# One expert scatter in place of two: the halves of a small item's output rows are summed on VectorE first

## What is computed

```python
D_MODEL, SEQ, N_EXPERTS, TOP_K, D_FF = 1024, 512, 32, 4, 1024

def _moe_sequence(h, w_router, b_router, w_gate_up, b_gate_up, w_down, b_down):
    logits = (jnp.einsum('ld,de->le', h, w_router) + b_router).astype(jnp.float32)
    top_val, top_idx = lax.top_k(logits, TOP_K)
    gates = jax.nn.softmax(top_val, axis=-1).astype(h.dtype)
    ...
    xs = h[tok]
    hgu = lax.ragged_dot(xs, w_gate_up, group_sizes) + b_gate_up[e_sorted]
    act = _clamped_swiglu(hgu)
    out = lax.ragged_dot(act, w_down, group_sizes) + b_down[e_sorted]
    out = out * gates.reshape(-1)[order][:, None]
    return jax.ops.segment_sum(out, tok, num_segments=L)
```

## Time and profile before

| | |
|---|---|
| median of 3 runs | 1970.95 us (1967.66 to 1971.95) |
| the profiled execution | 1965.19 us, span 1963.4 us |
| busy, share of the span | PE 95%, DVE 84%, ACT 69%, POOL 23% |
| items 0 to 33 | 743 to 1939 us of the span |
| mean granted TensorE clock | 0.976 of full speed |

### The profile page before, as it was taken

The page is one execution under the profiler, slowest core; times in us unless marked ns, Lnnn a source line. Parts: engine busy times, 40 slices in busy tenths (PEclk is TensorE's granted clock), DMA queues, the critical chain, the costliest instruction groups (busy, mean ns, idle before and its releaser), DMA issues.

```text
span 1963.4 us, 28736 instructions
## 1 busy us (share of the span) xinstructions
PE 1859.5 (95%) x8464; PEld 1450.4 (74%) x8464; DVE 1647.7 (84%) x1766; ACT 1357.9 (69%) x1777; POOL 455.4 (23%) x412
## 2 busy tenths in 40 slices
PE   6999999998989999999999999999999999999897
PEld 3657767787758887877777787677777778777775
DVE  6899987349765478989999998898898999989897
ACT  4556855224345525888788887888888888888885
POOL 6671000000000116412312311321222222212122
PEclk7999999999999998999999999999999999999999
DMA  8222225422110248999999999999999999999995
GB/s 321 81 107 86 86 79 190 138 83 91 34 43 23 47 155 266 355 376 377 368 403 375 373 376 381 366 367 387 368 363 404 374 383 375 391 383 358 399 380 209
DMA packets 134432, 526.22 MB, mean 268 GB/s; under 512 B 15809, under 2 KB 21089, under 8 KB 114208
## 3 DMA queue, kind: packets, MB, share of 16 engines
q1 hardware_dynamic: 118704, 492.45, 66.5%
q0 software_dynamic: 15664, 32.97, 6.5%
HBM read 512.76 MB, written 23.74 MB: 273 GB/s over the span
## 4 chain that ended last, share of the span: by engine, by line
PE 30%; DMA 12%; DVE 7%; ACT 5%; issue 5%; SPq 0%; ACTq 0%; DVEq 0%
PE ps L1135 25%; DMA ring<-in_w_gate_up 8%; DVE split L2826 4%; DMA arena<-in_w_gate_up 3%; PE ps L1184 3%; DVE arena_r L2826 2%; ACT arena_r L2024 2%; ACT split L2024 2%; ACT arena L2049 1%; PE ps L1088 1%; PE ps L1174 1%; DMA arena<-in_w_down 1%; DMA ring<-in_w_down 1%; DVE aTs L2770 0%; ACT arena L2060 0%
## 5 line engine op out<-in xcount | busy, mean ns | idle before, releaser
L1135 PE MATMUL ps<-split,xTs 128*128 128x512 f32 x2016 | 509.9, 401 | 20.3 <-DVE split L2826 14.7
L1135 PEld LDWEIGHTS ps<-split,xTs 128*128 128x128 f32 x2016 | 379.4, 191 | 120.3 <-DVE split L2826 33.4
L2826 DVE TENSOR_TENSOR split<-ring,split 128x2048 fp32r<-128x2048 f32 x136 | 308.2, 2295 | 42.6 <-ACT split L2024 36.9
L2826 DVE TENSOR_TENSOR split<-arena,split 128x2048 fp32r<-128x2048 f32 x136 | 308.7, 2286 | 4.0 <-ACT split L2024 3.6
L2024 ACT ACTIVATE split<-ring 128x1024 fp32r<-128x1024 f32 x272 | 272.5, 1057 | 51.4 <-DMA ring<-in_w_gate_up 47.3
L2024 ACT ACTIVATE split<-arena 128x1024 fp32r<-128x1024 f32 x272 | 272.5, 1052 | 44.8 <-DMA arena<-in_w_gate_up 16.1
L839 POOL DMA_INDIRECT y_rows<-arena,slots x50 | 108.1, 2162 | 336.4 <-issue 299.0
L1135 PE MATMUL ps<-arena_r,xTs 128*128 128x512 f32 x672 | 182.1, 405 | 0.9 <-DVE arena_r L2826 0.4
L1135 PE MATMUL ps<-arena_r,aTs 128*128 128x512 f32 x672 | 170.3, 398 | 0.0
L1135 PE MATMUL ps<-split,aTs 128*128 128x512 f32 x672 | 168.2, 396 | 1.0 <-DVE aTs L2886 0.3
L2826 DVE TENSOR_TENSOR arena_r<-ring,arena_r 128x2048 fp32r<-128x2048 f32 x68 | 157.1, 2311 | 3.6 <-ACT arena_r L2024 3.6
(11 more groups left out here) (480 smaller groups left out, 3128.1 us busy)
## 6 DMA issues: line engine op xcount, KB each, us to landing
ring<-in_w_gate_up SPq DMA_DIRECT2D x170, 1024.0 KB
arena<-in_w_gate_up SPq DMA_DIRECT2D x102, 1024.0 KB
arena<-in_w_down SPq DMA_DIRECT2D x102, 1024.0 KB
ring<-in_w_down SPq DMA_DIRECT2D x34, 1024.0 KB
ring<-in_w_in SPq DMA_DIRECT2D x23, 1024.0 KB
ring<-in_w_out SPq DMA_DIRECT2D x8, 1024.0 KB
ring<-in_mod_w SPq DMA_DIRECT2D x10, 512.0 KB, 9.2
ring<-in_mod_w SPq DMA_DIRECT2D x4, 1024.0 KB
```

Of the source, the lines that this page charges most:

```text
L1135: m = mm(ps[:, banks + q, :], lhs[:, x_, k, :], w[:, q * 512:(q + 1) * 512], start=start, stop=stop)
L2826: V.tensor_tensor(split_pair(1, p), chunk_pair(p), split_pair(0, p), ALU.subtract).then_inc(sig("lo_ready"), 1)
```

## The change

DVE gets an instruction, `join_halves`, behind the low part of pair 2 of every item that follows a small one. It multiplies PSUM rows 64 to 127 by the gates, adds `ysb` rows 0 to 63 (which ACT has written, now for 64 rows only, under the new semaphore `y_half`) and writes `ysb` rows 0 to 63. `y_ready` is counted up by DVE instead of ACT there. POOL issues one scatter of 64 slots where there were two, and no longer waits between them. In `item_rows`, `scattered` is therefore waited for at 16 per item. Items after a big item are as before.

Two things go with it. The loops of DVE and ACT are turned by one item: `big_item(0)`, whose predecessor is big, is taken out ahead, and the loop's body is now a small item and then a big one (PE's loop is as it was). And the load of `qk_rows` in the dense part counts on `tab_in`, so that DVE waits for one semaphore at 48 instead of two at 32 and 16.

```diff
-    def __init__(self, i, small, next_small, pairs, at, rows):
+    def __init__(self, i, small, next_small, pairs, at, rows, joined=None):
...
             def item_rows(it, before_small):
...
                 wait_alone(pool, sig("y_ready"), pool.to_reg(m + 0))
                 if before_small:
-                    scatter(0, HALF_SLOTS)
-                    wait_alone(pool, sig("scattered"), pool.to_reg(it.rows - 16))
-                    scatter(HALF_SLOTS, P)
+                    scatter(HALF_SLOTS)
                 else:
-                    scatter(0, P)
+                    scatter(P)
...
-                wait_alone(pool, sig("scattered"), pool.to_reg(it.rows + 0))
+                wait_alone(pool, sig("scattered"), pool.to_reg(m * 16))
...
-                    A(ysb, ps[:, 4:6, :].rearrange("p a b -> p (a b)"), ACT.Copy, scale=gate_s[:]).then_inc(sig("y_ready"), 1)
+                    if it.joined is not None:
+                        A(ysb[0:HALF_SLOTS, :], ps[0:HALF_SLOTS, 4:6, :].rearrange("p a b -> p (a b)"), ACT.Copy,
+                          scale=gate_s[0:HALF_SLOTS, :]).then_inc(sig("y_half"), 1)
+                    else:
+                        A(ysb, ps[:, 4:6, :].rearrange("p a b -> p (a b)"), ACT.Copy, scale=gate_s[:]).then_inc(sig("y_ready"), 1)
...
+                def join_halves():
+
+                    dve.wait_ge(sig("y_half"), it.joined + 0)
+                    V.scalar_tensor_tensor(ysb[0:HALF_SLOTS, :], ps[HALF_SLOTS:, 4:6, :].rearrange("p a b -> p (a b)"), gate_s[0:HALF_SLOTS, :],
+                                           ysb[0:HALF_SLOTS, :], ALU.mult, ALU.add).then_inc(sig("y_ready"), 1)
+
...
                 for p in range(4 if it.rows is None else 0, 6):
                     split_low(p)
+                    if p == 2 and it.joined is not None:
+                        join_halves()
...
             run(first_item())
+            run(big_item(0, False))
             with dve.Fori(0, LOOPS) as k:
-                run(big_item(k))
                 run(small_item(k))
-            run(big_item(LOOPS))
+                run(big_item(k + 1))
             run(small_item(LOOPS, True))
```

More of the change, by code:

```diff
@@ L110, with big_item @@
 class Item:
-    def __init__(self, i, small, next_small, pairs, at, rows):
+    def __init__(self, i, small, next_small, pairs, at, rows, joined=None):
         self.i, self.small, self.next_small = i, small, next_small
-        self.pairs, self.at, self.rows = pairs, at, rows
+        self.pairs, self.at, self.rows, self.joined = pairs, at, rows, joined
 def first_item():
     return Item(0, False, False, 0, None, None)
-def big_item(k):
-    return Item(k * 2 + 1, False, True, k * 2 * PAIRS + PAIRS, None, k * 48 + 16)
+def big_item(k, after_small=True):
+    return Item(k * 2 + 1, False, True, k * 2 * PAIRS + PAIRS, None, k * 48 + 16, k if after_small else None)
 def small_item(k, last=False):
@@ L133, in late_item @@
     return Item(j + (BEFORE_LATE - back), True, True, j * PAIRS + (BEFORE_LATE - back) * PAIRS,
-                j + (BEFORE_LATE - back - BIG), j * 32 + ((BEFORE_LATE - back) * 32 - BIG * 16))
+                j + (BEFORE_LATE - back - BIG), j * 32 + ((BEFORE_LATE - back) * 32 - BIG * 16), j + (BEFORE_LATE - back - BIG))
 FIRST_TAPS = (8, 7, 7, 9, 9, 9, 8, 6)
@@ L771, in _ @@
             pool.dma_start(tab[0:META, TC, :], a["tab"][T:L, :]).then_inc(sig("tab_in"), 16)
-            load_rows(qk_rows[:], "g_qk", 2 * P + E, sig("rows2_in"))
+            load_rows(qk_rows[:], "g_qk", 2 * P + E, sig("tab_in"))
             pool.wait_ge(sig("o_taken"), 8 * TC)
@@ L836, in _, with scatter @@
             store_pairs(8, TC * TOPK)
-            def scatter(lo, hi):
-                nc.gpsimd.indirect_dma_start(out=y_dram, out_offset=bass.IndirectOffsetOnAxis(idx_s[0:hi - lo, :], 0), in_=ysb[lo:hi, :], in_offset=None,
+            def scatter(n):
+                nc.gpsimd.indirect_dma_start(out=y_dram, out_offset=bass.IndirectOffsetOnAxis(idx_s[0:n, :], 0), in_=ysb[0:n, :], in_offset=None,
                                              bounds_check=last_token, oob_is_err=False, compute_op=ALU.add).then_inc(sig("scattered"), 16)
@@ L940, in _ @@
             load_slots(slot_g[0:HALF_SLOTS, :], 2, HALF_SLOTS, sig("slot_g_in"))
-            item_rows(big_item(0), False)
+            item_rows(big_item(0, False), False)
             def two_items(lo, hi):
@@ L2538, in _ @@
             weights_low(W_Z + 4)
-            dve.wait_ge(sig("tab_in"), 32)
-            dve.wait_ge(sig("rows2_in"), 16)
+            dve.wait_ge(sig("tab_in"), 48)
             def lo_of(low_, ps_, high_):
```

## The result

The changed kernel took **1954.83 us** in the median of 5 runs (1951.42 to 1955.26), the kernel before 1967.66 us in 5 runs beside it (1962.04 to 1971.95). The ratio is 0.9933, 95% interval [0.9914, 0.9951], so it is faster by 12.8 us. I had forecast 2.7 us of gain, 1968.3 us, and the range began at 1958 us: the forecast was wrong in size. A part of the distance to 1968.3 us is the base: the forecast was counted from 1970.95 us, 3.3 us above the kernel before as measured here; what was missed is 10.1 us of gain.

The account below looks back on a forecast made before the run. PE was taken to bound big items, with the DMAs in question for small ones. Joins in late items cost 3.6 us, saved DMA time gained 6.3 us: -2.7 us from 1970.95 us, forecast 1968.3 us, range 1958 to 1979 us.

Parts of the forecast that it names:

- The saved DMA time: Second scatters removed ahead of small items: 0.9 us of DMA time each, 0.45 us passing on for 14 pairs, 6.3 us gained.
- I take half: Share of 0.9 us DMA saving passing on to each small item behind: 0.45 us, ends 0 and 12.6 us in all.
- the hole: Some 30 us into a big item, 1592.4 to 1594.0 us: DMAs nearly run dry, about half the engines idle.
- The saving passes on in full: Rival: DMA bounds throughout, 14 times 0.9 is 12.6 us gained, less 3.6 us, giving 1962 us; chance 0.22.
- DMA: Bandwidth & Descriptors: Skill's lower price for the second scatter: 0.34 us of moving data for 0.15 MB, gain about 2.4 instead of 6.3 us.
- what late weights cost: PE's 12 waits for a late low part from DVE, 14.7 us in all, expected down to about 8.
- that no DMA is part of: PE's 25.6 us of waits, twice per small item, for ACT's copy ahead of `turn_sum`: a PE-ACT-PE round trip without DMA.
- POOL's wait: 0: POOL no longer waits for the first scatter before the second; nobody waits for its earlier slot list, so 0.
- The joins in big items: 0: 14 joins of 1.2 us on DVE fit 2.4 us slack at pair 3, repaid in waits for ACT: cost 0.
- joins on the path everywhere: Rival: all 17 joins at 1.2 us cost 20.4 us, less 6.3 us gained, giving 1985 us; chance 0.16.
- The joins in late items: 3.6 us lost: Three late items have no slack at pair 3, so the join's 1.2 us is on PE's path three times.
- the saving in DMA time does not help there: In the three late items saved DMA time gains nothing, as PE waits there for ACT.

## Why the prediction missed

**The saved DMA time (0.45 us for each of 14 pairs).** This is the first of two steps that failed. The engine time of a scatter was right, 0.96 for 0.9 us. "I take half", for what passes the hole, and only for 14 items, gave 6.3 us. Without the second scatter's rows alone the kernel gains 11.8 us (interval 7.7 to 15.7), and with them back in the change it loses 8.7 (about 4 to 13): 0.5 to 0.7 us for each of 17, or 53 to 72% of what the engines save. Two things made the term small. The dip was read too deep: "The digits in the hole are near 5", but the 16 digits of the earlier trace rows from 1592.4 us on have a mean of 6.9, so about a quarter of the engines' time is idle there and not half. By the prediction's own rule some three quarters of 0.9 us pass on then, 9.5 us for 14 items and 11.5 for 17, an estimate. And the three late items, put at nothing, gained too (see below). The rival "The saving passes on in full", 12.6 us, is inside the interval of the run without the rows, but 16.3 us, all that 17 transfers took, is not; its 1962 us was missed like the forecast, because of the other terms. That a tile has landed only when its last engine is done may let more through than the mean says; no run looks at single engines. The Trainium skill's page "Perfetto Trace Analysis", on identifying the most-contended engine, which says to optimize that one first, pointed the right way here, since more than half of the transfer time saved came out as time. The estimate from its page "DMA: Bandwidth & Descriptors", 2.4 us in all, is far under what these runs show.

**Which wait late weights end in.** The prediction named 14.7 us of PE's waits as "what late weights cost" and took the 25.6 us for ACT's copy as a round trip "that no DMA is part of". In the two profiles it was ACT's copies that came earlier, by 4.3 us in sum, while ACT waited 31 us less for DMAs; that the second is the reason for the first is shown at one item and by the order of the kernels, and not by a run of its own. The 14.7 us stayed. By the prediction's own test ("if PE's waits for late weights stay at 14.7 us") the mechanism would have been called dead while it worked.

**POOL's wait: 0.** This is the second step that failed. Without the wait and with all rows moved 4.7 us (interval 2.2 to 7.1) are gained. The run without the join has neither the wait nor the rows and gains 14.8 us (11.0 to 18.5), so within these intervals the two add up, 11.8 and 4.7. I had asked only who waits for POOL, and not when its transfer meets the weights' transfers.

**The clock.** Of the 11.8 us that the profiled items became shorter, 7.8 are less busy time of PE for the same matmuls, by the estimate above all of it from a better granted clock. I take it for a part of the other gains and not for one besides them, since no kernel here gained by it alone, but no run shows that; the run without rows had even fewer falls (PE busy 1017.1 us) and more idle time (50.9 us) at about the same total. A sum made of waits alone comes out too small.

**The joins in big items: 0.** Right, and for the reason given: slack at pair 3, repaid at DVE's waits for ACT. The rival that put joins on the path everywhere is excluded by the run without them; doubled, the join found the edge at pair 3, where the prediction had placed it, and one more at L2880.

**The joins in late items: 3.6 us lost.** PE did wait, 4.2 us in sum, yet with and without joins these items differ by 2.0 us in the profiles; PE's wait ahead of `turn_sum` is 2.5 us with joins and 4.1 us without, which gives 1.6 us back. And "the saving in DMA time does not help there" was wrong: without joins they fell from 98.8 to 95.1 us. PE's wait for ACT there was late weights again, in part:

```profile
ACT split L2024 <- DMA ring<-in_w_gate_up: 4.2, 5, 1.4
```

The changed kernel has no such row; of all weight tiles ACT waited 6.2 us there before (the four rows with a DMA) and 1.8 us after. And by 2.5 us PE was busy less in the late items (92.47 and then 90.00 us), at a clock of 0.97 and then 1.00.

**By the terms**, in us against before: rows -9 to -12, wait -5, joins 0 to +2, each give or take the intervals above; measured -12.8. The sum on record was -6.3, 0, +3.6.

## What to carry to other kernels

When PE waits for another engine's result, look at what that engine did just ahead: a short operation queued in order behind one that waits for a DMA is late because of the DMA, and the row in the list of waits won't say so. In a stretch in which the DMA share is 1.0, don't write saved transfer time off against a dip before its digits are added up: here a dip with a mean of 6.9 let half to three quarters of the saving through. Ask of a wait that goes away not only who waits for it, but when the next transfer now runs. And before adding work to a nearly full engine, find the exact point at which its consumer comes: here 2.4 us of slack took one operation of 1.2 us free of charge, and the next at 0.84 us.

## What the runs showed of the hardware

- An indirect transfer that POOL issues while DVE makes a low part is held until a low part ends. In the trace of before 43 of the 44 scatters that start during a low part end 1.3 to 1.5 us after the end of that one; for the two of the earlier trace rows it is 1.34 and 1.31 us after DVE's low parts end at 1567.24 and 1576.05. The Trainium skill's page "SBUF — State Buffer", in its section on the two separate sides, says that a DVE operation with two inputs in SBUF and a GpSimd operation that reads SBUF lock each other out for a whole instruction; low parts have two such inputs, and this trace agrees.
- That a scatter is held over several low parts is open. One that the join has released starts 0.8 to 1.0 us into the low part behind it, is let go 1.3 to 1.4 us after the third has ended, and so holds POOL for 7.0 to 7.2 us; with the join one pair later, where in a big item two low parts follow, it is 4.8 to 5.0 us. It happens without a join too, but seldom: 9.8 and 9.7 us in two late items of the run without joins (median 2.0 us), 11.7 and 10.7 us in the run without the rows.
- The join on 64 partitions takes 1.285 us, the like operation on 128 partitions 1.283 us: half the partitions save nothing. ACT's output copy takes 1.10 us for 64 partitions (L2043 at 1835.07) and 1.10 us for 128.
- Two scatters issued back to back cost 0.24% less than the same two with the landing of the first between them (0.9976 [0.9964, 0.9989] and 1.0003 [0.9991, 1.0014] of before).
